# A gate table for half of the tokens, put together in DRAM by GpSimd's indirect DMAs

## The reference, cut to what matters

```
q    = h @ w_query                       # 8 heads, two halves of 128
s1, s2 = q1 . sub_keys1, q2 . sub_keys2  # (token, head, 128) each
v1, i1 = top_k(s1, 16); v2, i2 = top_k(s2, 16)
top_s, pos = top_k(v1 + v2 over all pairs, 16)
idx   = i1 * 128 + i2 at pos             # 16 of 16384 experts per head
gates = softmax(top_s)
out[t] = sum over heads and k of gates * gelu(h[t] . expert_down[idx]) * expert_up[idx]
```

## Time and profile before

| | us |
|---|---|
| median of 3 runs | 2009.29 |
| lowest and highest | 2002.57, 2014.99 |
| span of the profiled execution, first to last instruction | 2015.2 |

### The profile page before, as it was taken

The page is one execution under the profiler, slowest core; times in us unless marked ns, Lnnn a source line. Parts: engine busy times, 40 slices in busy tenths (PEclk is TensorE's granted clock), DMA queues, the critical chain, the costliest instruction groups (busy, mean ns, idle before and its releaser), DMA issues.

```text
span 2015.2 us, 38041 instructions
## 1 busy us (share of the span) xinstructions
PE 1988.4 (99%) x14231; PEld 1842.9 (91%) x14231; DVE 1512.0 (75%) x2628; ACT 1025.4 (51%) x1394; POOL 0.2 (0%) x4
## 2 busy tenths in 40 slices
PE   9999999999999999999999999999999999999998
PEld 8888999999999888888899999999999998888886
DVE  6777779988885666666679665888888866666666
ACT  6741454455555444444546553544555554444444
POOL 0000000000000000000000000000000000000000
PEclk8999999999999999999999999999999999999999
DMA  8555767776566777777655655777766677777776
GB/s 302 177 200 190 280 202 243 237 246 200 186 187 217 238 243 238 243 240 242 208 170 168 189 165 179 226 237 229 235 196 186 187 226 238 244 238 242 239 245 189
DMA packets 136462, 440.85 MB, mean 219 GB/s; under 512 B 15136, under 2 KB 15392, under 8 KB 133920
## 3 DMA queue, kind: packets, MB, share of 16 engines
q1 hardware_dynamic: 118496, 406.84, 64.5%
q10 hardware_dynamic: 17856, 32.51, 4.4%
HBM read 403.64 MB, written 35.65 MB: 218 GB/s over the span
## 4 chain that ended last, share of the span: by engine, by line
PE 91%; DVE 5%; DMA 2%; ACT 1%; issue 1%; SPq 0%; DVEq 0%; ACTq 0%
PE ps L581 27%; PE ps L582 27%; PE ps L583 27%; PE ps L913 3%; DVE ring_lo L394 2%; PE ps L618 1%; DMA ring<-in_wq 1%; PE ps L631 1%; PE ps L761 1%; PE ps L889 1%; ACT ring_hi L388 1%; DMA arena<-in_w_ada 0%; DMA ring<-in_down 0%; DVE arena L1979 0%; DVE arena L1544 0%
## 5 line engine op out<-in xcount | busy, mean ns | idle before, releaser
L394 DVE TENSOR_TENSOR ring_lo<-ring,ring_hi 128x1024 fp32r<-128x1024 f32 x632 | 772.6, 1223 | 289.1 <-ACT ring_hi L388 285.3
L388 ACT ACTIVATE ring_hi<-ring 128x1024 fp32r<-128x1024 f32 x632 | 667.9, 1057 | 601.4 <-PE ps L583 496.1
L581 PE MATMUL ps<-h_hi,ring_lo 128*128 128x256 f32 x2816 | 801.6, 285 | 11.0 <-DVE ring_lo L394 8.6
L582 PE MATMUL ps<-h_lo,ring_hi 128*128 128x256 f32 x2816 | 789.0, 280 | 0.0
L583 PE MATMUL ps<-h_hi,ring_hi 128*128 128x256 f32 x2816 | 788.9, 280 | 0.0
L581 PEld LDWEIGHTS ps<-h_hi,ring_lo 128*128 128x128 f32 x2816 | 535.5, 190 | 15.0 <-issue 7.7
L582 PEld LDWEIGHTS ps<-h_lo,ring_hi 128*128 128x128 f32 x2816 | 532.8, 189 | 0.4 <-issue 0.2
L583 PEld LDWEIGHTS ps<-h_hi,ring_hi 128*128 128x128 f32 x2816 | 530.6, 188 | 0.0
L583 PE MATMUL ps<-ring_hi,w_hi 128*128 128x512 f32 x1024 | 399.0, 390 | 0.0
L581 PE MATMUL ps<-ring_hi,w_lo 128*128 128x512 f32 x1024 | 399.0, 390 | 0.0
L582 PE MATMUL ps<-ring_lo,w_hi 128*128 128x512 f32 x1024 | 399.0, 390 | 0.0
(11 more groups left out here) (300 smaller groups left out, 1331.4 us busy)
## 6 DMA issues: line engine op xcount, KB each, us to landing
ring<-in_down SPq DMA_DIRECT2D x256, 512.0 KB, 4.3
ring<-in_up SPq DMA_DIRECT2D x256, 512.0 KB, 4.0
ring<-in_w_in SPq DMA_DIRECT2D x72, 512.0 KB, 3.6
kept_z<-wf ACTq DMA_DIRECT2D x124, 256.0 KB, 3.2
xT<-kept_z SPq DMA_DIRECT2D x124, 256.0 KB, 4.2
arena<-in_w_ada SPq DMA_DIRECT2D x16, 1024.0 KB, 8.9
ring<-in_wq SPq DMA_DIRECT2D x32, 512.0 KB, 4.2
arena<-in_w_ada SPq DMA_DIRECT2D x16, 512.0 KB, 8.2
```

The costliest lines, as they stand in the source:

```text
L388: nc.scalar.activation(ring_hi[:, part_slot(m), :], ring[:, slot(m), :], ACT.Copy).then_inc(S("high"), 1)
L394: ns.tensor_tensor(ring_lo[:, part_slot(n), :], ring[:, slot(n), :], ring_hi[:, part_slot(n), :].bitcast(fp32), ALU.subtract)\
L581: mm(psum, s_lo, m_hi, start=start, stop=False)
L582: mm(psum, s_hi, m_lo, start=False, stop=False)
```

## The change: what it does, and its diff

For the first 128 tokens there are no gate groups. GpSimd gets a program. It fills a table in DRAM with zeros (`clear`, eight DMAs of 1 MB a layer, one at a time); the table has 128 rows of 16384 + 1024 entries, one row for each i1, and in a row the entry of i2 * 128 + token. VectorE works out the places of the first half's 128 entries per token (`places`), as soon as that half is selected, decoded and shared. Then `put` issues 128 indirect DMAs, each for one column k: 128 entries of 4 bytes, one of each token. The sixteen of head 0 write, those of the heads behind it add; after each head it waits for all sixteen. When the last gate group of the layer has been multiplied, `bring` reads the table into the first 128 columns of G in 32 DMAs of 256 KB, 4 rows of i2 each, the last ones first, one at a time; from the ninth on it also waits for VectorE's weighing.

The other half keeps its 32 groups, now two to a pair, one before each block, in pairs 38 to 53. VectorE's order becomes select 0, decode 0, shares 0, places, select 1, decode 1, shares 1; ScalarE takes the exponentials of the first half before pair 14 and of the second before pair 30. VectorE's weighing waits for the piece of the table that it needs.

```diff
+G_ROW = NKEYS * P + 1024
+G_FILL = 2048
+G_LOAD = 4
+CLEARS = NKEYS * P // G_FILL
+LOADS = NKEYS // G_LOAD
...
+        blank = sb("blank", [P, 512])
+        place = sb("place", [P, PH * TOPK], u32)
...
-        GPP = 3
+        GPP = 2
+        EXP_AT = (14, 30)
+        GROUPS = P // 4
+        GATED = GROUPS // GPP
 
         def gate_turns(p):
 
-            left = T // 4 - GPP * (p - TOP)
-            return (min(2, max(0, left)), min(1, max(0, left - 2)))
+            return (1, 1) if p < TOP + GATED else (0, 0)
...
-                for tt in range(TT):
-                    pe.wait_ge(S(f"pick_ready{l}"), tt + 1)
-                    for k in range(3):
-                        last = nc.tensor.transpose(PS[2 + tt][:, k * P:(k + 1) * P], pick[:, tt, k, :], ident)
-                    last.then_inc(S(f"pickT_ps{l}"), 1)
+                pe.wait_ge(S("pick_ready"), l + 1)
+                for k in range(3):
+                    last = nc.tensor.transpose(PS[3][:, k * P:(k + 1) * P], pick[:, 1, k, :], ident)
+                last.then_inc(S("pickT_ps"), 1)
                 down_pair(TOP - 1)
 
                 for p in range(TOP, TOP + 4):
-                    down_pair(p, None, (2, 1))
+                    down_pair(p, None, (1, 1))
                 with pe.Fori(0, 2) as q:
                     for p in range(TOP + 4, TOP + 10):
-                        down_pair(p, (q, 12), (2, 1))
-                for p in range(TOP + 16, PAIRS):
-                    down_pair(p, None, gate_turns(p))
+                        down_pair(p, (q, 12), (1, 1))
...
-                pe.wait_ge(S(f"pickT_ready{l}"), TT)
-                pe.wait_ge(S(f"g_evac{l}"), T // 4)
+                pe.wait_ge(S("pickT_ready"), l + 1)
+                pe.wait_ge(S(f"g_evac{l}"), GROUPS)
...
-                    t0 = extra * 4 + g * 4
+                    t0 = extra * 4 + P + g * 4
...
+                def exponentials(tt):
+                    act.wait_ge(S("gate_sub"), TT * l + tt + 1)
+                    A_(tv[:, tt, :, :], tv[:, tt, :, :], ACT.Exp).then_inc(S("gate_exp"), 1)
+
+                for p in range(EXP_AT[0]):
                     down_pair(p)
-                with act.Fori(0, 3) as q:
-                    for p in range(6, 12):
+                exponentials(0)
+                with act.Fori(0, 2) as q:
+                    for p in range(EXP_AT[0], EXP_AT[0] + 6):
                         down_pair(p, (q, 12))
-                for p in range(24, TOP - 8):
+                for p in range(EXP_AT[0] + 12, EXP_AT[1]):
                     down_pair(p)
-                for tt in range(TT):
-                    act.wait_ge(S(f"gate_sub{l}"), tt + 1)
-                    A_(tv[:, tt, :, :], tv[:, tt, :, :], ACT.Exp).then_inc(S(f"gate_exp{l}"), 1)
-                for p in range(TOP - 8, TOP):
+                exponentials(1)
+                for p in range(EXP_AT[1], TOP):
                     down_pair(p)
                 for p in range(TOP, TOP + 4):
-                    down_pair(p, None, (2, 1))
+                    down_pair(p, None, (1, 1))
                 with act.Fori(0, 2) as q:
                     for p in range(TOP + 4, TOP + 10):
-                        down_pair(p, (q, 12), (2, 1))
+                        down_pair(p, (q, 12), (1, 1))
...
+        @block.gpsimd
+        def _(pool):
+            g = nc.gpsimd
+
+            g.memset(blank[:, :], 0.0).then_inc(S("blank_ready"), 1)
+            pool.wait_ge(S("blank_ready"), 1)
+
+            def clear(l):
+
+                rows = A[f"g{l}"].rearrange("(p n) o -> p (n o)", p=P)
+                for k in range(CLEARS):
+                    part = rows[:, k * G_FILL:(k + 1) * G_FILL].rearrange("p (r n) -> p r n", n=512)
+                    g.dma_start(part, blank[:, None, :].to_broadcast([P, G_FILL // 512, 512]))\
+                        .then_inc(S("g_clear"), 16)
+                    pool.wait_ge(S("g_clear"), 16 * (l * CLEARS + k + 1))
+
+            def put(l):
+
+                pool.wait_ge(S("place_ready"), l + 1)
+                for h in range(PH):
+                    for k in range(h * TOPK, (h + 1) * TOPK):
+                        g.indirect_dma_start(
+                            out=A[f"g{l}"], out_offset=bass.IndirectOffsetOnAxis(ap=place[:, k:k + 1], axis=0),
+                            in_=pick[:, 0, 2, k:k + 1], in_offset=None,
+                            compute_op=ALU.bypass if h == 0 else ALU.add).then_inc(S("g_put"), 16)
+                    pool.wait_ge(S("g_put"), 16 * TOPK * (l * PH + h + 1))
+
+            def bring(l):
+
+                pool.wait_ge(S(f"g_ps{l}"), GROUPS)
+                rows = A[f"g{l}"].rearrange("(p n) o -> p (n o)", p=P)
+                for c in range(LOADS):
+                    if c >= 8:
+                        pool.wait_ge(S(f"wf_ready{l}"), 2 * (c - 8) + 1)
+                    i2 = (c - 1) % LOADS * G_LOAD
+                    g.dma_start(G[:, i2:i2 + G_LOAD, 0:P],
+                                rows[:, i2 * P:(i2 + G_LOAD) * P].rearrange("p (i t) -> p i t", t=P))\
+                        .then_inc(S("g_in"), 16)
+                    pool.wait_ge(S("g_in"), 16 * (l * LOADS + c + 1))
+
+            pool.wait_ge(S("block_used"), 20)
+            clear(0)
+            put(0)
+            bring(0)
+            pool.wait_ge(S("xa_evac"), 1)
+            clear(1)
+            put(1)
+            bring(1)
...
+                def shares(tt, signal):
+                    lows_to(max(lows, 2 * EXP_AT[tt] + RING))
+                    dve.wait_ge(S("gate_exp"), TT * l + tt + 1)
                     link(v.tensor_reduce(gsum[:, tt, :, 0], tv[:, tt, :, :], AX.X, ALU.add))
                     link(v.reciprocal(grec[:, tt, :, :], gsum[:, tt, :, :]))
                     link(STT(pick[:, tt, 2, :].rearrange("p (h k) -> p h k", h=PH), tv[:, tt, :, :], GATE_SCALE,
-                             grec[:, tt, :, :].to_broadcast([P, PH, TOPK]), ALU.mult, ALU.mult), f"pick_ready{l}")
+                             grec[:, tt, :, :].to_broadcast([P, PH, TOPK]), ALU.mult, ALU.mult), signal)
+
+                def places():
+                    where = past[:, 0, :]
+                    link(TS(where, pick[:, 0, 1, :], float(P), col("token", 0), ALU.mult, ALU.add))
+                    link(STT(where, pick[:, 0, 0, :], float(G_ROW), where, ALU.mult, ALU.add))
+                    link(v.tensor_copy(place[:, :], where), "place_ready")
+
+                select(0)
+                decode(0)
+                if l == 1:
+                    dve.wait_ge(S("g_put"), 16 * PH * TOPK)
+                shares(0, "dve_chain")
+                places()
+                select(1)
+                decode(1)
+                shares(1, "pick_ready")
                 lows_to(2 * TOP)
-                for tt in range(TT):
-                    dve.wait_ge(S(f"pickT_ps{l}"), tt + 1)
-                    groups = slice(tt * 32, (tt + 1) * 32)
-                    row = [PS[2 + tt][:, a * P:(a + 1) * P].rearrange("p (g t) -> p g t", t=4)[:, :, :, None]
-                           .to_broadcast([P, 32, 4, 2]) for a in range(3)]
-                    v.tensor_copy(sel16[:, groups, 0, 0, :, :], row[0])
-                    v.tensor_copy(sel16[:, groups, 0, 1, :, :], row[1])
-                    link(v.tensor_copy(sel16[:, groups, 1, 0, :, :], row[2]))
-                    link(TTn(sel16[:, groups, 1, 1, :, :], row[2], sel16[:, groups, 1, 0, :, :], ALU.subtract),
-                         f"pickT_ready{l}")
+                dve.wait_ge(S("pickT_ps"), l + 1)
+                groups = slice(GROUPS, 2 * GROUPS)
+                row = [PS[3][:, a * P:(a + 1) * P].rearrange("p (g t) -> p g t", t=4)[:, :, :, None]
+                       .to_broadcast([P, GROUPS, 4, 2]) for a in range(3)]
+                v.tensor_copy(sel16[:, groups, 0, 0, :, :], row[0])
+                v.tensor_copy(sel16[:, groups, 0, 1, :, :], row[1])
+                link(v.tensor_copy(sel16[:, groups, 1, 0, :, :], row[2]))
+                link(TTn(sel16[:, groups, 1, 1, :, :], row[2], sel16[:, groups, 1, 0, :, :], ALU.subtract),
+                     "pickT_ready")
...
                 def weigh_kept(j):
                     dve.wait_ge(S(f"act_done{l}"), NBACK + j + 1)
+                    dve.wait_ge(S("g_in"), 16 * (l * LOADS + 1))
                     weigh(j, wf[:, j % 2, :])
 
                 def weigh_back(j, at=None):
                     in_loop = 32 * at[0] if at else 0
                     dve.wait_ge(S(f"z_in{l}_{(j - 2) % 3}"), in_loop + 16 * ((j - 2) // 3 + 1))
+                    if j % 2 == 0:
+                        dve.wait_ge(S("g_in"), 8 * more_pairs(at) + 16 * (l * LOADS + j // 2 + 1))
                     weigh(j, z_back[(j - 2) % 3], at)
```

More of the change, by code:

```diff
@@ L37 @@
          ("a_log", 1), ("norm1", 8), ("conv_a_w", 32), ("conv_a_b", 8), ("b_a", 8), ("b_x", 8), ("lam", 8),
-         ("conv_b_w", 24), ("norm2", 8)]
+         ("conv_b_w", 24), ("norm2", 8), ("token", 1)]
 COL = {}
```

(52 more changed lines are left out.)

2 lines of the change are left out of this document (removed).

## The result

The kernel with the table takes 2229.4 us (median of 4 runs, 2224.0 to 2239.5) against 2010.5 for the kernel before on the same chip: a ratio of 1.110, 95% interval 1.105 to 1.114. It is 11% slower; 1982 was forecast, with 2066 as the upper end.

A forecast was written before the change was run, and what follows sets the result against it. TensorE, busy 1988.4 of 2015.2 us, was taken as the bound. Savings of 30.9 us less 4 of added transfers gave -27: 1988 on the profiled execution, carried over to 1982 for the median; range 1966 to 2066.

The forecast's parts named there:

- the price of a put: GpSimd's indirect DMAs: 1.05 us each, 134 + 26 = 160 us a layer, done at 512, 116 us early.
- the 1.95 from which the place decides: Us per put above which VectorE's wait for the table's first piece would set the time.
- the waits for a head's last landing: GpSimd's eight waits a layer, one landing of 3.2 us each: 26 us.
- the 275: Window in us for a layer's puts, from places ready at 352.2 to 627.6, before the table's first piece must land.
- A: Rival, late puts: VectorE waits for the table's first piece; 2066 us, at the upper bound 2252; chance 0.24.
- A's worked case: Each put waits for a VectorE low part: 2.27 us a put, 42 us late a layer, 2066 us.
- The groups: TensorE's gate products: 512 instead of 1024 fp16 products; with six transposes gone, 30.9 us saved.
- The pair with two groups: Gate stage, TensorE's pace: a pair of blocks with two gate groups takes 5.65 + 1.02 = 6.67 us.
- The places: VectorE's table positions for the first tokens: ready at 352.2, adding 0.9 us per layer.
- Clears, way back and puts beside the loads: DMA engines: clearing 1 us, way back 0.5 and puts 0.5 a layer, +4 us in all.
- rival B: Transfers crowd the block loads on the DMA engines: 16.5 us a layer, 2015 us, no change; chance 0.18.
- Rival C: GpSimd holds VectorE up 0.343 us at each put: 13 us late a layer, 2008 us; chance 0.10.

The follow-up runs named there:

- with 4096 bytes: Changed kernel with 4096 instead of 1024 bytes of room for GpSimd's DMA descriptors (dynamic_dma_scratch_size): 2095.2 us, ratio 1.042 to the kernel before.
- with four heads: Changed kernel, room 1024, with only four of the eight heads put into the table, the other four heads' gates left out: 1988.0 us, ratio 0.987.
- The run with 80 tokens: Changed kernel, descriptor room 4096, only 80 tokens through the table, 44 gate groups in pairs 38 to 59: 2028.8 us, ratio 1.008.
- the one with 64: Changed kernel, descriptor room 4096, only 64 tokens through the table, 48 gate groups in pairs 38 to 61: 2019.7 us, ratio 1.003.

## Why the prediction was wrong

**The step that failed is the price of a put.** "I take the geometric middle, 1.05 us" stood between an issue of 0.343 and a landing of 3.2. Measured: 2.9 without the waits for a head's landing, near the upper bound and past the 1.95 from which the place decides; 3.09 with them, where the forecast makes 1.25. Part by part of 395 us a layer:
- the put itself undisturbed, 0.96 writing and 1.54 adding, with the gaps: 16 x 0.96 + 112 x 1.54 + 36 = 224 us, where my 1.05 made 134;
- VectorE's low parts: 215.4 - (16 x 0.96 + 112 x 1.54) = 28 us;
- the stops: 122 us, a term that the sum did not have. I let "sixteen in flight" stand as the code has it, while GpSimd stopped after every one to three adding puts until they had landed;
- the waits for a head's last landing: 21.9 (26 forecast).

The first and the last term together, 246 us, would still have fitted into the 275; with VectorE's low parts they fill it, and the stops of 122 us are as much as the table was late (125). But the terms hang together: with 4096 bytes, where only some 32 us of stops were left, VectorE's part had grown to 46 us (233.7 - 187.8), and by my estimate the puts would have taken 293 us without any stop, still too long. Of the runs with all 128 tokens and all eight heads, only those that do not add were in time, or within 6.3 us of it.

**The rival that came true is A, in its place and not in its price.** VectorE's wait for the first piece of the table set the time, from 627.8 on (the forecast had the first weighing at 631.8) and 125 late a layer, where A's upper bound had 135 and 2252 us. But A's named price, a wait for VectorE's low part at each put, is the small term (1.83 instead of 1.54 even where the stops are mostly gone). The range ended at A's worked case although the page had no row of GpSimd at all; the bound of 3.2 us, which I had worked out, should have set the upper end.

**Held, point by point.** The groups: 512 products, 30.0 us less busy TensorE for 30.9. The pair with two groups, on ScalarE's timeline of after:

```profile
484.79 0.58 ACT L1247 ACTIVATE wf<-ps 128x512 f32<-128x512 f32 x1
...
491.48 0.58 ACT L1247 ACTIVATE wf<-ps 128x512 f32<-128x512 f32 x1
```

6.69 us for 6.67. The places were ready at 354.5 for 352.2. Clears, way back and puts beside the loads, VectorE's order and ScalarE's table loads: 1988 with four heads, where 1982 (1968 to 1989) was forecast for all that is on time. The clears and the way back were fewer packets than forecast: by their sizes in the trace, 8192 of 4096 bytes in all, where I had 8192 of 2 KB and 32768 of 512 B. So rival B (2015) falls: the DMA share rose from 0.78 to 0.86 in the selection stage at 244 GB/s, without a wait of TensorE, and a packet of an adding put took 27 ns (median), where one of 2 KB took 84. While the loads ran it was the puts that landed later. Rival C falls as well: it is VectorE that holds the put, not the other way round.

## What to carry to other kernels

Price an indirect DMA by the instruction, not by its bytes: on GpSimd one of 128 entries took 1.26 us writing and 1.84 adding (gap included), and an adding one of 64 entries 1.70. Then ask how many can be under way: with the small room GpSimd stopped after a few, mostly for 2 to 5 us, until all of them had landed. When the engine that is to do new work has no row in the profile, the upper bound belongs in the range. A wait that is moved (here SP's, behind the last gate group) can take the gain even when the work it guards is on time.

## What the runs showed of the hardware that was not expected

A put that adds has far more packets than one that writes: leaving out 224 adding puts' addition took 112 packets each from the queue, and leaving 128 adding puts out took (42752 - 24320) / 128 = 144 each, so 144 against 32, for the same 128 entries. The queue of the run with four heads:

```profile
q0 software_dynamic: 24320, 33.63, 6.5%
```

By their sizes in the trace these are 128 packets of 4 bytes for an adding put and 16 of 32 bytes for a writing one, and 16 more of 4 bytes for either.

TensorE's products have two spacings at the same granted clock of 1.00. In the kernel before, pairs without gate groups take 5.44 us in layer 0 until the first group, and 5.65 at the same place of layer 1 (ScalarE's evaluations):

```profile
336.49 0.58 ACT L1239 ACTIVATE wf<-ps 128x512 f32<-128x512 f32 x1
...
1339.62 0.58 ACT L1239 ACTIVATE wf<-ps 128x512 f32<-128x512 f32 x1
1345.28 0.58 ACT L1239 ACTIVATE wf<-ps 128x512 f32<-128x512 f32 x1
```

(The next one in layer 0 is the 341.93 of the earlier trace rows.) Layer 0 has 5.65 too, after its gate groups. The run with 80 tokens has 5.44 in both layers up to the groups, the one with 64 has 5.65 from the fourth pair of layer 0 on, before its first put. Over 37 pairs that is 8 us a layer; runs of the kernel before lay between 2003 and 2022. What sets it stays open.
